# Attention over two sets of keys: all four query blocks with the first set, then all four with the second

## What is computed

```
k_sel = min(K_SEL, n_sel)          # min(16, 512 // 64) = 8 blocks: all of them
ss = einsum(qb, kg) * scale        # selected keys ks
ps = softmax(where(ms, ss, NEG))
o_s = einsum(ps, vg)               # values vs
sw = einsum(qb, kw) * scale        # window keys kw
pw = softmax(where(mw, sw, NEG))
o_w = einsum(pw, vw)               # values vw
out = g[..., 0:1] * o_c + g[..., 1:2] * o_s + g[..., 2:3] * o_w
y = out * silu(z_nsa)              # then part of mixed @ w_out
```

## Time and profile before

| | us |
|---|---|
| three runs, median (lowest to highest) | 2585.16 (2584.24 to 2585.37) |
| the profiled execution, its own time | 2583.53 |
| its span (first to last instruction) | 2581.7 |
| TensorE busy in it | 2530.7 |
| VectorE busy | 1559.9 |
| ScalarE busy | 1141.3 |
| GpSimd busy | 1056.4 |
| attention stage of the second kind, first layer: 2043.9 to about 2164 | 120 |
| the same, second layer: about 2426 to 2546 | 120 |

### The profile page before, as it was taken

The page is one execution under the profiler, slowest core; times in us unless marked ns, Lnnn a source line. Parts: engine busy times, 40 slices in busy tenths (PEclk is TensorE's granted clock), DMA queues, the critical chain, the costliest instruction groups (busy, mean ns, idle before and its releaser), DMA issues.

```text
span 2581.7 us, 35308 instructions
## 1 busy us (share of the span) xinstructions
PE 2530.7 (98%) x12592; PEld 1980.0 (77%) x12592; DVE 1559.9 (60%) x2562; ACT 1141.3 (44%) x1980; POOL 1056.4 (41%) x440
## 2 busy tenths in 40 slices
PE   8999999999999999999999999999999999999998
PEld 6867667788888788676677888886887777887776
DVE  6248748743223462576487334226899866899765
ACT  3344444533223343444535233225437665347654
POOL 4432223354445444321243544443447612447612
PEclk9999999999999999999999999999999999999999
DMA  6321112233332243221132332332234211334211
GB/s 200 101 87 62 50 50 82 82 98 98 97 97 97 90 117 94 74 67 49 42 98 89 107 98 90 97 98 77 87 98 151 90 42 50 98 100 150 89 34 58
DMA packets 66896, 228.00 MB, mean 88 GB/s; under 512 B 8784, under 2 KB 8912, under 8 KB 66768
## 3 DMA queue, kind: packets, MB, share of 16 engines
q1 hardware_dynamic: 66192, 224.73, 27.6%
q10 hardware_dynamic: 576, 1.57, 0.2%
HBM read 216.57 MB, written 2.10 MB: 85 GB/s over the span
## 4 chain that ended last, share of the span: by engine, by line
PE 91%; DVE 4%; ACT 3%; issue 1%; POOL 1%; DVEq 0%; ACTq 0%; DMA 0%; SPq 0%
PE bank L412 25%; PE bank L414 24%; PE bank L413 24%; PE bank L635 3%; PE bank L605 3%; PE bank L621 2%; PE bank L611 1%; PE bank L918 1%; PE bank L1308 1%; POOL w_lo L508 1%; ACT work L673 1%; PE bank L892 1%; DVE work L716 1%; PE bank L1280 1%; PE bank L1279 1%
## 5 line engine op out<-in xcount | busy, mean ns | idle before, releaser
L508 POOL TENSOR_TENSOR w_lo<-w_raw,w_hi 128x1024 fp32r<-128x1024 f32 x404 | 1012.1, 2513 | 1516.0 <-ACT w_hi L421 1509.2
L412 PE MATMUL bank<-x_hi,w_hi 128*128 128x512 f32 x1984 | 798.8, 403 | 22.1 <-DVE x_lo L2735 10.4
L414 PE MATMUL bank<-x_hi,w_lo 128*128 128x512 f32 x1984 | 775.6, 391 | 0.0
L413 PE MATMUL bank<-x_lo,w_hi 128*128 128x512 f32 x1984 | 774.3, 390 | 0.0
L421 ACT ACTIVATE w_hi<-w_raw 128x1024 fp32r<-128x1024 f32 x400 | 419.1, 1055 | 437.7 <-PE bank L414 356.7
L412 PEld LDWEIGHTS bank<-x_hi,w_hi 128*128 128x128 f32 x1984 | 373.7, 188 | 116.1 <-issue 22.8
L414 PEld LDWEIGHTS bank<-x_hi,w_lo 128*128 128x128 f32 x1984 | 373.2, 188 | 80.2
L413 PEld LDWEIGHTS bank<-x_lo,w_hi 128*128 128x128 f32 x1984 | 374.3, 189 | 71.2 <-issue 1.0
L412 PE MATMUL bank<-rhs_hi,w_hi 128*128 128x512 f32 x624 | 244.4, 392 | 0.0
L413 PE MATMUL bank<-rhs_lo,w_hi 128*128 128x512 f32 x624 | 242.9, 389 | 0.0
L414 PE MATMUL bank<-rhs_hi,w_lo 128*128 128x512 f32 x624 | 242.7, 389 | 0.0
(11 more groups left out here) (456 smaller groups left out, 3375.2 us busy)
## 6 DMA issues: line engine op xcount, KB each, us to landing
w_raw<-w SPq DMA_DIRECT2D x404, 512.0 KB, 3.5
work<-proj SPq DMA_DIRECT2D x60, 64.0 KB, 2.1
ln_in<-x SPq DMA_DIRECT2D x4, 512.0 KB, 7.5
out<-residual SPq DMA_DIRECT2D x8, 256.0 KB, 2.1
p_raw<-p ACTq DMA_DIRECT2D x2, 512.0 KB, 3.5
silu_z_nsa<-b_q SPq DMA_DIRECT2D x16, 64.0 KB, 2.4
work<-b_q SPq DMA_DIRECT2D x16, 64.0 KB, 2.8
silu_z_nsa<-b_kc SPq DMA_DIRECT2D x8, 64.0 KB, 2.0
```

Source lines behind the costliest of these rows:

```text
L412: nc.tensor.matmul(out, wh, xh, start=first, stop=False)
L413: nc.tensor.matmul(out, wh, xl, start=False, stop=False)
L414: S.last = nc.tensor.matmul(out, wl, xh, start=False, stop=last)
L508: S.nc.gpsimd.tensor_tensor(S.wl[s][:, :], S.raw[s][:, :], S.wh[s][:, :].bitcast(F32), ALU.subtract).then_inc(S.lo_ready[s], 1)
```

## The change

Within a tile the pairs now count br, then b: first all four blocks with `ks` (widths 128, 256, 384, 512), then all four with `kw` (the same again). The bank of a tile is opened once, by its first pair, and closed once, by its last. The first pair of a tile that uses split queries is now number 1 of its tile instead of number 2, so the high halves of the queries are made after pairs 6, 13 and 20 instead of 7, 13 and 21, and the low halves after 7, 14 and 21 instead of 8, 14 and 22. The number of instructions and the size of each stay the same on every engine; the queues of GpSimd and SyncE are the same row by row.

```
--- before.py
+++ after.py
@@ -789,7 +789,7 @@
 
     pairs = []
     for n in range(4 * QB * 2):
-        t, b, br = n // (2 * QB), n // 2 % QB, n % 2
+        t, br, b = n // (2 * QB), n // QB % 2, n % QB
         w = (b + 1) * P
         name, v = (("ks", S.vtok["s"]), ("kw", S.vtok["w"]))[br]
 
@@ -807,7 +807,7 @@
         gate = S.gate[:, :].rearrange("p (b e t c) -> p b e t c", b=QB, e=2, t=B_REP)[:, b, :, t, 1 + br]
         pairs.append(Pair(S, n, b, key,
                           (S.causb[:, :], b * P), lambda e, x, v=v: v[:, x * P + e * HD:x * P + (e + 1) * HD],
-                          (S.ps[3], S.X[3])[t % 2], gate=gate, first=None if br else compressed, begins=not br, ends=br == 1))
+                          (S.ps[3], S.X[3])[t % 2], gate=gate, first=None if br else compressed, begins=not br and b == 0, ends=br == 1 and b == QB - 1))
     return pairs
 
 
@@ -2186,7 +2186,7 @@
                 return [(S.mc_y, L * 4 + 4), (S.cpt_copied, L * 2 + 2)]
             if what == "values" and n % (2 * QB) == 0 and n >= 4 * QB:
                 return [(S.mn_y, L * 4 + n // (2 * QB) - 1)]
-            if what == "keys" and n > 2 * QB and n % (2 * QB) == 2:
+            if what == "keys" and n > 2 * QB and n % (2 * QB) == 1:
                 return [(S.nsa_lo, nsa_split(L, f"q{n // (2 * QB)}"))]
             return []
 
@@ -2368,8 +2368,8 @@
                 used(L, B_PW2 + n // 2)
             if n in (5, 6):
                 key_hi(("ks", "kw")[n - 5])
-            if n in (7, 13, 21):
-                query_hi((7, 13, 21).index(n) + 1)
+            if n in (6, 13, 20):
+                query_hi((6, 13, 20).index(n) + 1)
             if n in (1, 3):
                 for t in range(n - 1, n + 1):
                     act.wait_ge(S.mc_y, L * 4 + t + 1)
@@ -2668,8 +2668,8 @@
                 out_add(S, dve, L, i, *divmod(r, 2))
             if n in (6, 7):
                 key_lo(("ks", "kw")[n - 6])
-            if n in (8, 14, 22):
-                query_lo((8, 14, 22).index(n) + 1)
+            if n in (7, 14, 21):
+                query_lo((7, 14, 21).index(n) + 1)
             if n > 8 and n % 8 == 2:
                 mix(n // 8 - 1)
             if n > 8 and n % 8 == 4:
```

## The result

The changed kernel takes **2605.23 us** (median of three runs, 2603.77 to 2608.38) against 2585.16 before: ratio 1.008, 95% interval 1.0067 to 1.0094. It is slower, by 0.8%. The forecast was 2603.0, the range 2590 to 2607. Two executions (one of the kernel before beside run 1, 2819 us, and one in run 5, 3552 us), at a mean granted clock of 0.85 and 0.72 of full speed, are left out of the ratios.

What follows compares the result with a forecast made beforehand. TensorE, busy 98% of the span, was taken as the bound. Terms of 5.3, 2.0, 0.9, 0.3 and 0.4 gave 8.9 us a layer, 17.8 for two; with 2583.53 and 1.63 offset, 2603.0 us, range 2590 to 2607.

Steps and rivals of the forecast that it cites:

- Term B: Tiles 1 to 3: VectorE's `mix_lo` waits behind GpSimd's split, so TensorE waits 1.76 us per tile, 5.3 us a layer.
- Term C: First tile: a gapless 10 us GpSimd train catches gate and scalings of pairs 4 and 5; 2.0 us a layer.
- Term D: Before pair 9: the first split query's low half comes late, a wait of 1.5 instead of 0.6; 0.9 us a layer.
- pair 2: Wait at pair 2 grows by 0.3 us: pair 1 is 256 wide instead of 128; bounds 0 and 0.6.
- end: Stage end: values(30) two blocks narrower, less to do while the last `mix_lo` waits for the last split; 0.4 us.
- The lead of 0.05: Tiles 1 to 3: GpSimd's split starts 0.05 us before VectorE's `mix_lo`, so VectorE was taken to wait.
- Rival 1: VectorE's `mix_lo` keeps its place before the split; the rest stays, 7.2 us in all, 2592.4 us; chance 0.16.
- The bank opened once: 0: Opening a tile's bank once changes flags alone and costs 0 us.
- the casts, splits and weight loads: 0: These keep their order, each slot 12 us ahead of its use, so they cost 0 us.
- the time can only move by TensorE's waits: First step: no TensorE instruction is added or removed, so only its waits in the two attention stages can change time.
- the sign that all busy times but VectorE's stay within a few us: Expected in the new profile: busy times of all engines except VectorE change by no more than a few us.
- rival 3: First to start always wins; a first-tile scaling waits too, up to 1.7 us more a layer, 2606 us; chance 0.06.

Runs made afterwards that it cites:

- run 1: The changed kernel again, with nothing altered: 2607.84 us, ratio 1.0082 to the kernel before.
- run 5: The changed kernel with `mix_lo` ahead of `out_add` and the cast behind pair 4 moved behind pair 5: 2588.42 us, ratio 1.0018.
- run 2: The changed kernel with VectorE making `mix_lo` before `out_add` at pairs 12, 20 and 28: 2593.15 us, ratio 1.0032.
- run 4: The kernel before with a drain, a small memset and a drain on VectorE ahead of `mix_lo` at pairs 12, 20 and 28: 2600.44 us, ratio 1.0061.
- run 6: run 5 plus the first query's half ahead of the second key's and a stage's last cast behind the last `mix_hi`: 2585.54 us, ratio 1.0005.
- run 11: The changed kernel once more, unaltered, on the same chip as run 10: 2604.67 us, ratio 1.0083.
- run 10: The changed kernel with 18 small matmuls on TensorE ahead of the wait before pairs 15, 23 and 31: 2603.21 us, ratio 1.0073.

## Why the prediction was right, and where it was not

The sum for a layer was 8.9 us. In the profile in which all six tiles lost (run 1) TensorE's waits grew by 8.6 in a layer, and term by term:

| term | forecast | measured | shown by |
|---|---|---|---|
| B, collision, three tiles | 3 x 1.76 = 5.3 | 3 x 1.69 = 5.1 | runs 2, 4 |
| C, first tile | 2.0 | 0.85 + 1.52 - 0.59 = 1.8 | run 5 |
| D, first split query | 0.9 | 1.55 - 0.64 = 0.9 | run 6, in part |
| pair 2 | 0.3 | 1.29 - 0.74 = 0.55 | not tried |
| end | 0.4 | 0.61 - 0.33 = 0.3 | run 6 |

**Term B.** The lead of 0.05 was right to within 0.014 (0.036 to 0.058), and so was the choice that VectorE loses at it. (Its price, by its own numbers, is 8.59 - 6.85 = 1.74, not 1.76.) It was nearer a tie than I made it: of 24 such meetings in four profiles VectorE won two, by 1.7 us of TensorE each. Rival 1 (VectorE keeps its place) happened, in 1 tile in 12. Run 2 is rival 1 made by hand, at 2593.15 where it was priced at 2592.4.

**Term C.** The train's place was right to 0.2 us, its mechanism too. Instead of one wait of 2.7 us there were two, 2.4 in all: 0.85 before turn(5), which I had not counted as a place, and 1.52 before pair 7. From this I took off 0.7, the longer of the two waits in the earlier trace rows; the one that stands in this place is the other, 0.59. The near-tie named in it, whether VectorE slips in ahead of the last split, went to VectorE for the first of the two scalings (it started 0.26 ahead) and against it for the second, within 0.01 of the split's start in all four profiles.

**Term D** was exact as a sum. Of its cause the runs show 0.6 us to be the key's half that stands ahead; for the rest the chain of pair 8 is argued from run 6's timeline, not tried.

**Small ones.** The wait at pair 2 was sized too low, within its bounds. "The bank opened once: 0" and "the casts, splits and weight loads: 0" stand: GpSimd's busy time is 1056.4 in both profiles, and run 6, with all of this in it, is level with the kernel before.

**The step that failed** is the first: "the time can only move by TensorE's waits". By it a wait costs what it lasts. I never asked what TensorE's clock does behind a wait of 1.7 us, and the sign that all busy times but VectorE's stay within a few us missed TensorE's 5.0. The waits before were all below 0.8, and the clock held. In the profiled executions of the changed kernel it fell two or three times in the stages, 5.1 us in all in each of the three profiles. In the first profile 18.85 less 13.5 of waits inside the stages leaves 5.3, and its 10.2 us at half clock explain 5.1 of them.

**Luck.** The forecast came within 2.2 us since two errors partly cancel: 17.8 of waits were forecast, 14.1 came in that execution (one collision was won, which is 1.7, and the wait before pair 9 of the second layer shrank to 0.2 behind the slow stretch, which is 1.35), and 5.3 came on top. The forecast's own bounds in the chances, 2597 to 2605, miss the median by 0.2, and rival 3's 2606 is nearer to it than 2603.0; only the waits tell the two apart. The upper bound of 2607 had no half clock in it, and of the twelve executions of the changed kernel here (the result, runs 1 and 11) six lie above it, up to 2608.65.

The rule of the Trainium skill that the prediction weighed (SBUF — State Buffer, section "SBUF: two separate sides": who starts first keeps the lock) held in 22 of the 24 meetings, whose leads are 0.041 us and more. It does not hold in the two that VectorE won at 0.036 and 0.041 behind. Rival 3, that rule at its word in the first tile, did not come: the further wait of 1.7 us stands in none of the profiles. On the clock, the Trainium skill (TensorE: Matmul & The Clock Gate, section "Why this matters for your kernels") warns of idle gaps a good deal longer than those here. The measurement decides: a stretch at half clock came behind waits of 1.5 to 1.9 us in 11 cases of 42.

**What stays open.** Why one such wait is followed by half clock and the next is not; where the clock fell in the executions of run 2 that were not profiled; and why the wait at pair 2 grew by 0.55 instead of 0.3, for which nothing was tried.

## What to carry to other kernels

Before an order is changed, list the instructions of VectorE and GpSimd that exclude each other and how far apart they start: a lead of a tenth of a microsecond on the right side was worth 5 us a layer here, and at most 0.4 us of delay, put in by hand, cost 16 us where the reordering cost 20. Put first on VectorE what needs both inputs from SBUF, and behind it what reads a bank, when a long GpSimd instruction is due. And price a new wait of a busy TensorE above its own length if it is as long as those here (1.5 to 1.9 us): one in four was followed by half clock, at 1.7 us or more. Behind the waits of 1.3 us none was.

## What the runs showed of the hardware

- TensorE's granted clock fell from 2.4 to 1.2 GHz behind waits of 1.5 to 1.9 us, in 11 of 42 cases (nine of 22 at 1.68 to 1.86 us, two of 20 at 1.52 to 1.56), for 3.4 us or twice that, at the cost of 1.7 us for each 3.4. 18 small matmuls of 1.19 us in all, put into the wait (0.57 left idle), were followed by no fall in six cases of six, where the same waits unfilled had nine in 22.
- `mix_lo` started up to 0.041 us behind the split by the profile and still went first; at 0.041 it also lost once, and at every larger lead. The second scaling of pair 5, with one input tile, lost even where it started 0.007 and 0.009 ahead of the split (run 10). So starts in the profile within some 0.04 us of each other don't tell who goes first.
- A VectorE instruction that comes behind the split ends 0.55 us after it, whether it came 0.05 or 0.30 late.
- Three memsets of one column delayed what follows on VectorE by 0.02 to 0.03 us together; one with a drain before and behind it, by 0.34 to 0.41.
